# Regrouping the recurrent core and the attention around a filler stream, and moving pool evictions from ScalarE to VectorE

## The reference

```python
u_pool, q, k, v, p_rw, gate_logits = split(rms_norm(x) @ w_in[l])
b_pool = pool_mixer(u_pool, pool_w[l], pool_scale[l])     # 4 groups of 128 columns, windows 2, 4, 8, 16
b_da   = diff_attention(q, k, v, lam, ...)                # 4 heads, two softmaxes each, masked by chunks of 64
b_rw   = rwkv7_mixer(p_rw, ...)                           # 8 heads of 64, a recurrence over time
gates  = sigmoid(gate_logits)                             # 3 x 1024 columns
x = x + (sum_n gates_n * (branch_n @ w_branch[l, n])) @ w_out[l]
x = x + conv_glu_ffn(rms_norm(x), ...)
```

## Time and profile before

| | us |
|---|---|
| runs shown (3), lowest, median, highest | 2700.55, 2702.24, 2708.22 |
| the profiled execution, its own time | 2703.13 |
| its span, first to last instruction | 2701.2 |
| PE busy | 2646.8 (98%) |
| DVE busy | 1803.7 (67%) |
| ACT busy | 1134.5 (42%) |
| POOL busy | 290.2 (11%) |

### The profile page before, as it was taken

How to read it: one execution, slowest core, us unless ns; L and a number is a source line. 1 busy time by engine, 2 the same in 40 slices (tenths; PEclk the granted TensorE clock), 3 DMA queues, 4 the chain that set the end, 5 groups by cost and what they waited for, 6 DMA issues and landing times.

```text
span 2701.2 us, 55911 instructions
## 1 busy us (share of the span) xinstructions
PE 2646.8 (98%) x24551; PEld 2419.1 (90%) x24551; DVE 1803.7 (67%) x2828; ACT 1134.5 (42%) x1844; POOL 290.2 (11%) x175
## 2 busy tenths in 40 slices
PE   8999999999999999999999999999999999999998
PEld 8988998999999999988898899999987788878886
DVE  7744336556888746934335555888836998887887
ACT  6323334624333324423324634333323355466664
POOL 1211122130000000311122221000000000010001
PEclk9999999999999999999999999999999999999999
DMA  4211322364333343211222253333332322399996
GB/s 150 75 42 35 99 91 65 106 200 153 128 132 127 133 136 112 87 50 35 78 87 84 73 192 122 118 128 138 125 106 75 110 79 106 143 388 387 393 393 246
DMA packets 114203, 373.19 MB, mean 138 GB/s; under 512 B 13072, under 2 KB 14240, under 8 KB 113568
## 3 DMA queue, kind: packets, MB, share of 16 engines
q1 hardware_dynamic: 88848, 303.97, 32.3%
q10 hardware_dynamic: 18592, 41.92, 4.4%
q0 software_dynamic: 6512, 23.62, 2.3%
HBM read 336.44 MB, written 31.94 MB: 136 GB/s over the span
## 4 chain that ended last, share of the span: by engine, by line
PE 85%; DVE 9%; ACT 4%; DMA 1%; issue 1%; POOL 0%; DVEq 0%; ACTq 0%; SPq 0%; POOLq 0%
PE PS L316 83%; DVE ARENA L1218 1%; DVE HR L482 1%; DVE ARENA L846 0%; ACT ARENA L408 0%; PE PS L3273 0%; PE PS L1425 0%; DVE RINGR L311 0%; DVE ARENA L848 0%; DVE H L492 0%; DMA RING<-wts 0%; DVE ARENA L813 0%; ACT ARENA L410 0%; DVE ARENA L815 0%; DVE WR L3262 0%
## 5 line engine op out<-in xcount | busy, mean ns | idle before, releaser
L316 PE MATMUL PS<-HR,HIGHR 128*128 128x264 f32 (+1 forms) x2976 | 845.8, 284 | 0.0
L316 PEld LDWEIGHTS PS<-HR,HIGHR 128*128 128x128 f32 x2976 | 561.8, 189 | 0.8
L316 PE MATMUL PS<-XR,HIGHR 128*128 128x264 f32 (+2 forms) x1760 | 546.7, 311 | 6.8 <-ACT STAGE L612 5.3
L300 ACT CAST HIGHR<-RING 128x1024 fp32r<-128x1024 f32 (+2 forms) x340 | 330.6, 977 | 289.0 <-DMA RING<-wts 109.4
L316 PE MATMUL PS<-XR,RINGR 128*128 128x264 f32 (+1 forms) x1568 | 446.1, 284 | 0.0
L316 PE MATMUL PS<-HH,HIGHR 128*128 128x264 f32 (+2 forms) x1472 | 422.5, 287 | 1.4 <-DVE RINGR L311 1.4
L316 PE MATMUL PS<-HH,RINGR 128*128 128x264 f32 (+2 forms) x1472 | 421.5, 286 | 0.0
L311 DVE TENSOR_TENSOR RINGR<-RING,HIGHR 128x1024 fp32r<-128x1024 f32 (+2 forms) x272 | 308.2, 1138 | 117.1 <-ACT HIGHR L300 117.0
L316 PEld LDWEIGHTS PS<-XR,HIGHR 128*128 128x128 f32 x1760 | 332.5, 189 | 40.5 <-issue 20.2
L316 PE MATMUL PS<-ARENA 64*64 64x64 f32 (+10 forms) x7946 | 296.7, 240 | 11.4 <-DVE ARENA L1218 2.9
L316 PEld LDWEIGHTS PS<-XR,RINGR 128*128 128x128 f32 x1568 | 297.1, 189 | 0.0
(11 more groups left out here) (445 smaller groups left out, 5090.2 us busy)
## 6 DMA issues: line engine op xcount, KB each, us to landing
RING<-wts SPq DMA_DIRECT2D x324, 512.0 KB, 3.6
ARENA<-wmoe SPq DMA_DIRECT2D x204, 512.0 KB, 6.9
RING<-wts SPq DMA_DIRECT2D x52, 256.0 KB, 3.1
gates<-STAGE ACTq DMA_DIRECT2D x48, 264.0 KB, 4.3
ARENA<-gates ACTq DMA_DIRECT2D x48, 264.0 KB, 2.9
ys<-RING ACTq DMA_DIRECT2D x16, 512.0 KB, 6.9
RING<-wts SPq DMA_DIRECT2D x16, 384.0 KB, 3.1
ys<-STAGE POOLq DMA_DIRECT2D x8, 512.0 KB, 6.1
```

What stands on the lines that cost most here:

```text
L300: e.copy(k.highR[:, hs, 0:n], k.ring[:, i % NRING, 0:n]).then_inc(*k.s["hi"].done(i))
L316: return e.matmul(out, lhsT, rhs, start=start, stop=stop, skip_group_check=True)
```

## The change

Eight edits, in both layers:

1. Core, PE: the filler steps of tiles 1 to 4 stand in eight calls (3, 2, 1, 1, 1, 1, 1, 1) in place of eleven of one. The transposes of K move from before C to behind A8. The banks of each product are fixed. The parts of Y and H that don't need U are issued ahead of XX and of GF. For tile 0 the four matmuls of `unread` go.
2. Core, DVE: TI is made from the bank of AT4 and not from its copy in SBUF, and stands ahead of DI.
3. Attention: two units of distance, EE and AB threefold, one call of four steps for each unit; ACT copies the sum out ahead of the cast (`behind`).
4. Pool inputs and outputs are evicted by DVE, not ACT.
5. Gates 13 to 19 have their low parts made by DVE, not POOL.
6. The value tiles go in an order in which those in the banks of the last projection come last.
7. After the column sums, the `fill` of the third on ACT goes behind the fourth.
8. Low-rank products: one table, loaded ahead, serves tanh and sigmoid; a cast goes behind the sigmoids.

```diff
@@ gate_pe
-                     ("gate_pe", (l, i, 1)), lo="lo_pool")
+                     ("gate_pe", (l, i, 1)), lo="lo_dve" if 13 <= i < 20 else "lo_pool")
@@ pool_in_pe, pool_out_pe
-                k.banks.emptied_by(6 + hi, 1, "pool_act", (l, g, "in", hi))
+                k.banks.emptied_by(6 + hi, 1, "pool_dve", (l, g, "in", hi))
...
-        k.banks.emptied_by(6 + hi, 1, "pool_act", (l, g, "out", hi))
+        k.banks.emptied_by(6 + hi, 1, "pool_dve", (l, g, "out", hi))
@@ fill_act
-        elif what == "pool_in":
...
-            e.activation(k.UU[i][:, 16 + a:16 + a + ln], k.PS[:, 6 + hi, 0:ln], ACT.Copy,
-                         scale=k.col("pool_scale", i, l)).then_inc(*s["pool_act"].done((l, i, "out", hi)))
+    if behind:
+        behind()
     high_parts(k, e, w, slabs + AHEAD - 1)
@@ fill_dve
     while k.fill_at["dve"] < f.log[at][1]:
         what, g, hi = f.events[k.fill_at["dve"]]
         k.fill_at["dve"] += 1
+        a, ln = HALVES[T][hi]
+        if what == "pool_in":
+            w.wait_ge(*s["pool_pe"][l, g, "in", hi])
+            w.wait_ge(*s["pool_dve"][l, "zero"])
+            e.tensor_copy(k.UU[g][:, 16 + a:16 + a + ln], k.PS[:, 6 + hi, 0:ln]).then_inc(
+                *s["pool_dve"].done((l, g, "in", hi)))
+        elif what == "pool_out":
+            w.wait_ge(*s["pool_pe"][l, g, "out", hi])
+            w.wait_ge(*s["pool_dve"][l, g, "pooled"])
+            e.tensor_scalar(k.UU[g][:, 16 + a:16 + a + ln], k.PS[:, 6 + hi, 0:ln], k.col("pool_scale", g, l), None,
+                            MUL).then_inc(*s["pool_dve"].done((l, g, "out", hi)))
         if what != "pool_in" or hi == 0:
             continue
@@ inputs_act
         if i == 2:
+            e.preload_act_table_set("sigmoid_and_others")
+            k.both = False
             w.wait_ge(*V[l, "mixed", 0])
-            k.both = False
             e.activation(k.WA[0:64, :], k.WA[0:64, :], ACT.Tanh).then_inc(*A.done((l, "tanh")))
...
         if 3 <= i <= 4:
-            if i == 3:
-                high_parts(k, e, w, k.slabs.index["wa2", l] + AHEAD)
             for n in (2 * i - 6, 2 * i - 5):
...
+            if i == 3:
+                high_parts(k, e, w, k.slabs.index["wa2", l] + AHEAD)
@@ core_pe
-        turn(2, k.Kf, banks.place(w, key("turn"), 2))
-        beside()
+        beside(3)
...
-        beside()
+        if not j:
+            beside(3)
+
         w.wait_ge(*V[key("C")])
         w.wait_ge(*A[key("D")])
-        product("AT4", k.bC, k.bD, 0, away, "core_act", key("AT4"))
-        product("A4", k.bD, k.bC, 0, away, "core_dve", key("A4"))
-        b = banks.place(w, key("NV"), 2)
+        product(0, "AT4", k.bC, k.bD, 0, away, "core_dve", key("TI"))
+        product(1, "A4", k.bD, k.bC, 0, away, "core_dve", key("A4"))
+        beside(2)
+
+        b = place(2, "NV")
...
-        product("A8", k.bAT, k.bA, away, 0, "core_dve", key("A8I"))
+        product(1, "A8", k.bAT, k.bA, away, 0, "core_dve", key("A8I"))
+        turn(2, k.Kf, place(2, "turn"))
...
+        by = place(2, "Y")
+        for q in range(4):
+            state_part(quarter(by, q), tok(q, k.VT), lambda r, g: k.bQk[r, 4 * g + q, 0:cw], q == 0)
         if j:
             w.wait_ge(*V[key("EE")])
             w.wait_ge(*A[key("X")])
             w.wait_ge(*V[key("X")])
-            wide("XX", k.bEEI, k.U2, 1, 0)
-            beside()
+            wide(0, "XX", k.bEEI, k.U2, 1, 0)
+        bh = place(1, "H")
+        w.wait_ge(*A[key(("turned", 2))])
+        for q in range(4):
+            state_part(quarter(bh, q), tok(q, k.KT), tok(q, k.VT), q == 0)
+        beside(1)
+
+        bg = place(0, "GF")
...
-        if not j:
-            unread(k, e, by, 2)
@@ core_dve
-        w.wait_ge(*A[key("D")])
-        plus_one("DI", k.bDI, cut(k.bD))
...
         w.wait_ge(*A[key("AT4")])
-        plus_one("TI", k.bTI, cut(k.bAT))
+        plus_one("TI", k.bTI, halves("AT4"))
+        w.wait_ge(*A[key("D")])
+        plus_one("DI", k.bDI, cut(k.bD))
@@ attention
+def value_tiles(k, l):
+    b = k.banks.at[l, "qk", 7]
+    return sorted(range(5), key=lambda j: b <= j < b + 2)
...
-    for u in range(len(UNITS) + 1):
-        if u < len(UNITS):
-            scores(u)
-        if u:
-            fill(2 if u < len(UNITS) else 5)
-            turned(u - 1)
-            fill(2)
-            summed(u - 1)
+    last = len(UNITS) - 1
+    for u in range(last + 1):
+        scores(u)
+        if u == 1:
+            fill(2)
+        if u >= 2:
+            turned(u - 2)
+            fill(4)
+            summed(u - 2)
+    for u in (last - 1, last):
+        fill(2)
+        turned(u)
+        fill(last + 1 - u)
+        summed(u)
...
         power_act(k, e, w, "att_act", (l, "subln", h), k.KN[:, h], k.pv(at[l, "subln", h]), 1.0 / 128, 1e-5)
-        fill()
+        if h != 2:
+            fill()
+    fill()
```

More of the change, by code:

```diff
@@ L915, in core_pe, with place @@
         rows = lambda c: slice(64 * c, 64 * c + cw)
+        def place(pair, name, nb=2):
+            banks.next = 2 * pair
+            return banks.place(w, key(name), nb)
         def turn(kind, src, b):
@@ L922, in turn, with product, wide @@
             banks.emptied_by(b, 1, "core_act", key(("turned", kind)))
-        b = banks.place(w, key("turns"), 2)
+        def product(pair, name, left, right, of, to, *by):
+            b = place(pair, name)
+            along(k, e, j, b, left, right, of, to).then_inc(*P.done(key(name)))
+            banks.emptied_by(b, 2, *by)
+        def wide(pair, name, left, right, of, to):
+            b = place(pair, name)
+            along(k, e, j, b, left, right, of, to).then_inc(*P.done(key(name)))
+            banks.emptied_by(b, 1, "core_act", key(name))
+            banks.emptied_by(b + 1, 1, "core_dve", key(name))
+        b = place(0, "turns")
         w.wait_ge(*V[l, "centring"])
@@ L927, in core_pe @@
         turn(1, k.BH, b + 1)
-        b = banks.place(w, key("A"), 2)
+        b = place(1, "A")
         if j:
@@ L942, in core_pe @@
         banks.emptied_by(b, 2, "core_dve", key(("turned", 3)))
[L943 removed]
+        b = place(2, "AT")
         across(k, e, j, b, 0, k.BH, k.AH, away)
@@ L1012, in core_pe @@
         banks.emptied_by(b + 2, 2, "core_dve", key("E" if j else "R"))
[L1013 to L1021, removed]
         last = "R"
         if j:
+            product(2, "ET", k.bO, k.bQ, 1, 0, "core_act", key("ET"))
+            beside(1)
             w.wait_ge(*V[key("ETI")])
@@ L1031, in core_pe, with state_part @@
             w.wait_ge(*A[key("ET")])
-            product("EE", k.bE, k.bET, 0, 1, "core_dve", key("EE"))
-            beside()
+            product(1, "EE", k.bE, k.bET, 0, 1, "core_dve", key("EE"))
+            last = "XX"
+        U = k.U3 if j else k.U1
+        def state_part(place, left, right, start):
+            for c in ck:
+                for g in range(2):
+                    x = right(rows(c), g)
+                    b, at = place(c)
+                    ins = mm(e, k.PS[ch(g), b, at:at + x.shape[-1]], left(rows(c), g), x, start, True)
+            return ins
+        u = lambda q, part: lambda r, g: U[r, 4 * g + q, 64 * part:64 * part + 64]
+        pb = lambda q, a, n: lambda r, g: k.PB[r, 4 * g + q, a:a + n]
+        tok = lambda q, x: lambda r, g: x[r, q, ch(g)]
+        quarter = lambda b, q: lambda c: (b + c, 64 * q)
+        by = place(2, "Y")
+        w.wait_ge(*V[key("Qk")])
+        w.wait_ge(*A[key(("turned", 0))])
+        for q in range(4):
+            state_part(quarter(by, q), tok(q, k.VT), lambda r, g: k.bQk[r, 4 * g + q, 0:cw], q == 0)
+        banks.emptied_by(by, 2, "core_act", key("Y"))
+        if j:
             w.wait_ge(*V[key("EE")])
@@ L1048, in core_pe @@
         w.wait_ge(*A[key(("turned", 1))])
[L1049 to L1055, removed]
-                x = right(rows(c), g)
-                b, at = place(c)
-                ins = mm(e, k.PS[ch(g), b, at:at + x.shape[-1]], left(rows(c), g), x, start, True)
-            return ins
-        gf = lambda q, x: lambda c: (bg + c, 128 * q + 64 * x)
-        quarter = lambda b, q: lambda c: (b + c, 64 * q)
-        u = lambda q, part: lambda r, g: U[r, 4 * g + q, 64 * part:64 * part + 64]
-        pb = lambda q, a, n: lambda r, g: k.PB[r, 4 * g + q, a:a + n]
-        tok = lambda q, x: lambda r, g: x[r, q, ch(g)]
         for q in range(4):
@@ L1289, in core_pool @@
     for j in range(5):
-        for i in range((9 if j else 6) + len(chunks(j)[0])):
+        for i in range(6 + len(chunks(j)[0])):
             fill()
@@ L1514, in soft, with emptied, copied @@
         ins.then_inc(*A.done((l, "exp", u)))
-    for u in range(len(UNITS) + 1):
-        if u:
-            fill()
-            turned(u - 1)
-        if u < len(UNITS):
-            soft(u)
-        if u:
-            j, h = UNITS[u - 1]
-            t0, n = TILES[j]
-            fill()
-            w.wait_ge(*P[l, "summed", u - 1])
```

(25 more changed lines are left out.)

142 lines of the change are left out of this document (60 added, 82 removed).

## The result

The changed kernel takes 2738.4 us (median of 4 runs, 2735.0 to 2740.8) against 2703.0; the ratio is 1.013, interval 1.0117 to 1.0143. It is slower by 35 us. The forecast was 2719, range 2697 to 2732: the sign was right, the size half of it, and the time lies outside the range.

The account below looks back on a forecast made before the run. The prediction took PE, busy 98% of the span, to set the time. Gains of 15.4 us and eviction losses of 32.3 turned 2703.1 into 2720.0 profiled, 2719 median, range 2697 to 2732.

Parts of the forecast that it names:

- The evictions' waits: Column sums to merge: PE stands for pool output evictions queued behind DVE's running mean; 16.2 us lost per layer.
- The meeting with POOL: Same stretch: POOL's slab work delays DVE's mean, raising the first wait from 3.4 to 5.0 us, the second to 4.7.
- The sum: Whole kernel: 2703.1 - 15.4 + 32.3 = 2720.0 us for the profiled execution, 2719 as the median.
- all it can lose is new waits: Whole kernel: matmuls stay but for `unread`, so only waits and changes of stream can be won, only new waits lost.
- The core: Recurrent core: fewer filler calls, covered waits, tile 1's DI and `unread` save 4.2 us per layer.
- the meeting of POOL and AI: Core, tile 3: a slab's cast of 2.4 us on POOL meets AI on DVE, costing about 0.6 us.
- The attention: Attention: 17 filler calls fewer save 1.5 us per layer, less new waits; net gain 0.6.
- the value order: Value tiles: the reordering removes a PE wait of 0.84 us but adds a little before later scores; gain 0.5 per layer.
- The column sums' wait and the low-rank table: Column sums: one wait for L612 goes, 1.2 us per layer; low-rank products: table load and cast leave PE's path, 1.2.
- the evictions are covered: Rival, column sums to merge: DVE's idle time hides the evictions, gains stand alone, 2687 us; chance 0.18.
- loss and gain cancel: Rival, whole kernel: no meetings with POOL, small merge part, core wins nearly all its waits; about 2704 us; chance 0.15.
- The waits for "issue": Rival, core: a run of 80 products without filler stands 1.4 us in eight tiles, 11 more, 2730 us; chance 0.12.

Follow-up runs that it names:

- k1: The changed kernel with the pool product evictions given back to ScalarE, all else as changed; 2698.3 us, ratio 0.9985 to the kernel before.
- k2: The kernel before with only the pool evictions moved to VectorE; 2745.0 us, ratio 1.0165.
- k3: The changed kernel, evictions still on VectorE, but each running mean queued behind the previous pool output's evictions; 2710.6 us, ratio 1.0031.
- k4: The changed kernel with unread products added on TensorE in the four places per layer where it waits for VectorE; 2720.9 us, ratio 1.0075.
- k5: The kernel before with only the four functions of the core as changed; 2702.2 us, ratio 0.9997.
- k7: The changed kernel, pool evictions on ScalarE, with four filler steps instead of three per place in the core's first tile, one fewer ahead of NV elsewhere; 2699.1 us.
- k10: The changed kernel, pool evictions on ScalarE, with two filler steps moved into the first tile's run of thin products from NV to Y2; 2694.7 us, ratio 0.9977.

## Why the prediction was right in sign and wrong in size

Its sum for the profiled execution was 2720.0; it came to 2740.3. Step by step:

- **The evictions' waits: right.** Forecast 5.0, 4.7, 4.2 and 2.3, 16.2 per layer; measured 4.27, 1.82 + 3.73, 3.85 and 1.88, 15.55. The mechanism is shown by k1, k2 and k3. The meeting with POOL is in the rows as well: the two sums at 498.57 took 2.73, not twice 0.73. The forecast had no wait of 1.82: it stands ahead of pool output 1's second half, for the eviction of input 2 behind a low part of 2.53.
- **The failed step: "The sum", and the sentence that it rests on, "all it can lose is new waits".** It has no term for TensorE's clock: it priced a wait at its own length, on a trace whose clock stood at 1.00 in these stretches, and took the core's matmuls to last as long as before. The stretch to the merge grew by 21.5, its waits by 15.55, 1.17 of an old one went, and 1.46 are moved steps, so 5.6 us are none of these. The clock of 0.86 over 62.12 us is (1 - 0.86) x 2 x 62.12 = 17 us at the lower level, some of it in waits; half of 17 is the most it could cost, 8.7. Behind the merge's start 15 more matmuls stand 0.22 apart, 1.5 us. k4 confirms the term by taking it away. That is 7.1 per layer, 14 for both. Some 5 of these came back in the stages behind, which no term had and no run here takes apart, so that from the column sums on some 9 of the 20 us missed remain.
- **The core is the other half of the miss, some 11 of the 20 us, by the same missing term.** Forecast 4.2 less per layer; from its first tile to its end it took 169.51 for 165.22 in layer 0 and 166.23 for 166.08 in layer 1, and the stage behind it was 1.0 shorter in each. The first tiles alone are 4.1 and 2.7 longer, at a clock of 0.82 in both layers. The trace of before held a warning: its first tile stood at 0.95. At an equal clock the gain is nearly as forecast: in k3's trace layer 0's core has as little time at the lower level as before's, and is 3.1 shorter. Its tiles 1 to 3:

```profile
149.25:181.74 32.49, 30.02 (x884) 27.26 (x883) 14.57 (x24) 10.36 (x18) 4.77 (x2) 1.00 0.16 49
181.74:212.38 30.64, 29.76 (x884) 27.13 (x883) 14.57 (x24) 9.90 (x18) 2.37 (x1) 1.00 0.10 30
212.38:243.75 31.37, 30.20 (x884) 27.42 (x883) 16.56 (x24) 11.06 (x19) 4.43 (x2) 1.00 0.18 46
```

Tile 2 is the forecast's 30.6. Tile 3 has the meeting of POOL and AI, a wait of 0.67, and so gained nothing, as its own term said (0.65 less 0.6). Tile 1 was to be 29.5, a misreading: that came from a stretch of 31.39 which ended before the tile did. Before, the tile took 33.99; less 0.65 and 1.2 that is 32.1, and 32.49 was measured, with 1.72 on "issue" where 1.33 was before.
- **The attention: the mechanism right, the gain smaller than both terms.** From its first scores to the column sums 107.98 became 105.93 in layer 0, 2.05 less; 1.46 of that are the two moved steps, so 0.6 is won, for a forecast of 0.6 and 0.5 more for the value order. A new wait of 0.29 stands ahead of the second unit's scores.
- **The column sums' wait and the low-rank table: right.** One L612 wait per layer is gone; the core starts at 116.09 in place of 117.77, 1.7 for a forecast of 1.2.
- **Rivals.** That the evictions are covered is out, and that loss and gain cancel is out as well. The waits for "issue" grew by 2.6 us (5.5 for 2.9), not 11, and none of them stands in the run from C to A4; what they wait for isn't shown.

The range left out its own case of more loss than the waits. I gave 26 to 32 us to the loss and had bounded each wait, not what follows a wait.

## What to carry to other kernels

Where one engine is busy for 98% of the span, a wait of it cost its length and then some of the matmuls behind it at half the clock: here 1.4 us more behind a wait of 4.27, and 44 us for 30 of waits (k2). Look at the granted clock of each stretch before and after, not only at the waits; a stretch at 1.00 says nothing of the price once a wait is put there. And when an eviction moves to another engine, ask what stands ahead of it in that queue, for the bank's next writer waits for all of it.

## What the runs showed that was not expected

- Added products that nobody reads made the kernel 17.5 us faster (k4), 10.8 us of it, in its trace, by holding the clock where TensorE had stood.
- The clock can fall with no wait at all, in a full step behind a run of products of 16 rows (131.2 us of after), and it does so in some executions of the same code and not in others: the stretch 110 to 190 us, with the same first tile, had 0.89 in after and k5, 0.91 in k1, 0.98 in k3 and k4. The runs of k1, 2689 to 2704, stand almost in the order of their clock; that these falls in the first tile are what spreads them fits that, but only one execution of each kernel has a trace.
- A change of order that is worth 5 to 8 us at an equal clock measured as nothing (k5, 0.9997). What in the first tile's order makes the clock fall more often stays open: k7 leaves it possible that more steps help, and k10 shows that cutting the longest thin run is not enough by itself.
